# The second product of an MLP by Strassen's scheme, with the squared tiles kept in DRAM

## What is computed

```python
def sq_relu_mlp(h, w1, w2):
    return jnp.square(jax.nn.relu(h @ w1)) @ w2     # h 1024x1024, w1 1024x4096, w2 4096x1024
...
    xl = xl + g2_l * sq_relu_mlp(modulate(rms_norm_2(xl, norm2_g[i]), sh2_l, s2_l), mlp_w1[i], mlp_w2[i])
return rms_norm_2(xl, final_g)
```

## Time and profile before

| | |
|---|---|
| median of 3 runs | 2042.74 us (2037.37 to 2042.86) |
| profiled execution: span, first to last instruction | 2035.5 us |
| TensorE busy | 2002.3 us, 98% of the span |
| VectorE busy | 1062.4 us, 52% |
| ScalarE busy | 814.5 us, 40% |
| GpSimd busy | 775.0 us, 38% |

### The profile page before, as it was taken

How to read it: one execution, slowest core, us unless ns; L and a number is a source line. 1 busy time by engine, 2 the same in 40 slices (tenths; PEclk the granted TensorE clock), 3 DMA queues, 4 the chain that set the end, 5 groups by cost and what they waited for, 6 DMA issues and landing times.

```text
span 2035.5 us, 26356 instructions
## 1 busy us (share of the span) xinstructions
PE 2002.3 (98%) x10210; PEld 1682.8 (83%) x10210; DVE 1062.4 (52%) x1903; ACT 814.5 (40%) x1365; POOL 775.0 (38%) x482
## 2 busy tenths in 40 slices
PE   9999999999999999999999999999999999999997
PEld 7988988988987888888878877788788888888886
DVE  6154455436555465654589978897541211112125
ACT  5423331343434622132365575753544333222311
POOL 4511111112121344353359857794444444222220
PEclk9999999999999999999999999999999999999998
DMA  5301101110112596774345432332223332111112
GB/s 187 104 22 52 46 29 52 48 47 32 48 47 87 182 316 241 244 272 161 110 186 186 175 102 97 96 94 91 92 84 104 98 99 83 50 44 52 52 42 83
DMA packets 69566, 215.64 MB, mean 106 GB/s; under 512 B 7857, under 2 KB 8241, under 8 KB 69313
## 3 DMA queue, kind: packets, MB, share of 16 engines
q1 hardware_dynamic: 55472, 188.26, 27.5%
q10 hardware_dynamic: 13968, 25.70, 3.7%
HBM read 184.56 MB, written 29.36 MB: 105 GB/s over the span
## 4 chain that ended last, share of the span: by engine, by line
PE 60%; DVE 3%; ACT 2%; issue 2%; POOL 1%; POOLq 0%; DVEq 0%; ACTq 0%
PE B L1519 34%; PE B L1698 24%; PE B L1789 1%; DVE HB L2242 1%; POOL WL L2774 0%; PE B L1725 0%; POOL CO L2819 0%; DVE B L2242 0%; DVE RES L2242 0%; DVE TM L2242 0%; ACT CO L2191 0%; PE B L1683 0%; PE B L1772 0%; ACT HB L1914 0%; ACT RES L2146 0%
## 5 line engine op out<-in xcount | busy, mean ns | idle before, releaser
L1519 PE MATMUL B<-HB,WH 128*128 128x512 f32 x2976 | 929.4, 400 | 5.5 <-ACT HB L1914 3.1
L1519 PEld LDWEIGHTS B<-HB,WH 128*128 128x128 f32 x2976 | 546.9, 188 | 124.8 <-issue 15.2
L2774 POOL TENSOR_TENSOR WL<-RAW,WH 128x1024 fp32r<-128x1024 f32 x164 | 394.2, 2407 | 591.2 <-ACT WH L1914 590.1
L1519 PE MATMUL B<-HB,WL 128*128 128x512 f32 x1488 | 562.3, 391 | 1.8 <-POOL WL L2774 1.8
L1914 ACT ACTIVATE WH<-RAW 128x1024 fp32r<-128x1024 f32 x205 | 215.3, 1055 | 454.1 <-DMA RAW<-wall 434.1
L1519 PEld LDWEIGHTS B<-HB,WL 128*128 128x128 f32 x1488 | 279.8, 188 | 62.9 <-POOL WL L2774 3.4
L2772 POOL TENSOR_TENSOR WL<-RAW,WH 128x512 fp32r<-128x512 f32 x82 | 113.5, 1408 | 317.2 <-ACT WH L1914 317.1
L2242 DVE SCALAR_TENSOR_TENSOR RES<-B,modv,RES 128x512 f32<-128x512 f32 x144 | 105.2, 747 | 200.4 <-PE B L1698 176.7
L2242 DVE SCALAR_TENSOR_TENSOR B<-UP,vec,B 128x512 f32<-128x512 f32 x308 | 208.1, 746 | 0.0
L1698 PE MATMUL B<-HIDH,WH 128*128 128x512 f32 x512 | 185.4, 395 | 1.4 <-DVE RES L2242 1.4
L1698 PE MATMUL B<-HIDL,WH 128*128 128x512 f32 x512 | 182.4, 389 | 0.0
(11 more groups left out here) (247 smaller groups left out, 2598.7 us busy)
## 6 DMA issues: line engine op xcount, KB each, us to landing
RAW<-wall SPq DMA_DIRECT2D x204, 512.0 KB, 3.5
...
WH<-parts SPq DMA_DIRECT2D x32, 512.0 KB, 3.2
WL<-parts SPq DMA_DIRECT2D x32, 512.0 KB, 4.1
RES<-xT SPq DMA_DIRECT2D x16, 512.0 KB, 8.3
...
OI<-oscr SPq DMA_DIRECT2D x16, 512.0 KB, 5.2
parts<-WH SPq DMA_DIRECT2D x16, 512.0 KB, 5.2
```

The costliest lines, as they stand in the source:

```text
L1519: i = pe.matmul(bank, a[:, ks], hb(part, k, h), start=k == 0 and n == 0, stop=k == 7 and n == 2)
L2774: i = po.tensor_tensor(lo, raw, hi.bitcast(F32), ALU.subtract)
```

## The change

The hidden tiles of a group form a 2x2 block matrix B: two by two channel tiles, by the two halves of the tokens. A weight unit holds, for each such pair, four 128x128 quarters A. For groups 0 to 6 the product of A and B is made by the Winograd form of Strassen's scheme, with 7 block products (`part`) in place of 8. Group 7 stays as it was.

- `hid` on ScalarE takes the relu into `RL`, which frees the bank, and the square into one of 4 buffers `HR`; `hid_store` sends it to DRAM (`hscr`), a DMA issued by ScalarE. `hid_lo` is gone. All 32 first-product tiles of one half are made, then all 32 of the other, and only then comes the second product of all groups. The last four tiles of the first half (`FILL`) stand beside the norm of the second half, where one group stood.
- `hq_load` on SyncE's queue reads the squares back, 2 MB a group in four DMAs.
- `op_sum` on GpSimd makes the sums of B quarters, 8 a group. `operand` splits each of the 14 operands of a group: high copy on ScalarE, low subtraction on VectorE.
- `w_sum` on VectorE makes four sums of A quarters of each weight unit, 4 instructions of 128x256. ScalarE copies the sums' high part (`SUMH`, 128x1024), GpSimd subtracts the low part (`SUML`, 128x1024), behind the unit's own split.
- `part_out` on VectorE adds each block product, or a running sum of them in its bank, to `RES`: 6 a unit, 24 a group. The second product of the seven stays in a bank of its own (2 to 5) over groups 0 to 6.

```diff
+TERMS = {1: ("A11", "B11"), 2: ("A12", "B21"), 3: ("S4", "B22"), 4: ("A22", "T4"), 5: ("S1", "T1"), 6: ("S2", "T2"), 7: ("S3", "T3")}
+INTO = {1: (0, 0), 2: (0, 0), 6: (0, 1), 3: (0, 1), 5: (1, 1), 7: (1, 1), 4: (1, 0)}
+    plan += [("w1", i, 0) for i in range(4 * HG - FILL)]
+    plan += [("pw2", f, 1) for f in range(8)] + [("w1", i, 0) for i in range(4 * HG - FILL, 4 * HG)]
+    plan += [("w1", i, 1) for i in range(4 * HG)]
+    plan += [("w2", g, j, 2) for g in range(HG) for j in range(4)]
...
+    for n in range(N):
+        if n % 4 == 0:
+            for _ in ahead_of:
+                pass
+            ahead_of = operands_ahead(n // 4 + 1)
+        order = [(n, 1), (n - 1, 7), (n, 5), (n, 2), (n - 1, 4), (n, 6), (n, 3)]
+        for place, (u, m) in enumerate(order):
+            if u >= 0:
+                part(u, m)
+                for w in waiting:
+                    part_out(*w)
+                waiting = [(u, m)]
+            unit_ahead(n, place)
+            at_ = 7 * (n % 4) + place
+            late_slots[0] = at_ >= 24
+            if at_ >= 3 and at_ % 4 != 2:
+                next(ahead_of, None)
...
+                for r in range(2):
+                    for i, (wt, op) in enumerate(((hi, OPH[x]), (hi, OPL[x]), (lo, OPH[x]))):
+                        p = pe.matmul(bank, wt[:, c:c + 128], op[:, :], start=opens and r == 0 and i == 0,
+                                      stop=r == 1 and i == 2, skip_group_check=True)
...
-                ac.activation(BANKS[b], RL[:, :], ACT.Square).then_inc(sig["hid_sq"], 1)
-                copy(HID[i % NH][0][h][:, :], BANKS[b]).then_inc(sig["hid_hi"], 1)
+                ac.activation(RL[:, :], BANKS[b], ACT.Relu).then_inc(taken[b], 1)
+                ac.activation(HR[at_][:, :], RL[:, :], ACT.Square).then_inc(sig["hid_sq"], 1)
+            def hid_store(i, h):
+                n = hid_n[i, h]
+                w.wait_ge(sig["hid_sq"], n + 1)
+                ac.dma_start(hscr[i, :, h * 512:(h + 1) * 512], HR[n % NHR][:, :]).then_inc(sig[f"d_back{n % NHR}"], 16)
...
+            def operand(q, m):
+                x = SLOT_OF[q, m]
+                w.wait_ge(sig["op_hi"], nth["operand", q, m])
+                if m == 5:
+                    w.wait_ge(sig["op_sum"], nth["op_sum", q, 6])
+                elif m == 6:
+                    w.wait_ge(sig["op_sum"], nth["op_sum", q, 4])
+                tt(OPL[x][:, :], raw_operand(q, m), OPH[x][:, :].bitcast(F32), ALU.subtract).then_inc(sig["op_lo"], 1)
+            def w_sum(q, s):
+                w.wait_ge(sig[f"d_raw{q % NW}"], 16 * raw_n[q])
...
+                if s == "S1":
+                    i = tt(two, quarter(raw, "A21"), quarter(raw, "A22"), ALU.add)
...
+            def part_out(g, j2, m):
+                stt(rh(f, h), BANKS[b], modcol[:, 40 + f:41 + f], rh(f, h), ALU.mult, ALU.add).then_inc(taken[b], 1)
...
+                if q in SUMMED:
+                    n = SUMMED[q]
+                    w.wait_ge(sig["s_hi"], n + 1)
+                    po.tensor_tensor(SUML[n % 3][:, :], SUMR[n % 3][:, :], SUMH[n % 3][:, :].bitcast(F32),
+                                     ALU.subtract).then_inc(sig["s_lo"], 1)
+            def op_sum(q, m):
+                to = OPT[SLOT_OF[q, m]][:, :]
+                wait_operand_slot(w, q, m)
+                wait_hq(w, q)
+                if m == 5:
+                    i = po.tensor_tensor(to, hq(q, "B12"), hq(q, "B11"), ALU.subtract)
...
+            def hq_load(q):
+                if q > 1:
+                    w.wait_ge(sig["op_lo"], nth["operand", q - 2, 7])
+                for k, i in enumerate(tiles):
+                    sp.dma_start(HQ[q % 2][k][:, :], hscr[i, :, :]).then_inc(sig[f"d_scr{q % 2}"], 16)
```

More of the change, by code:

```diff
@@ L128, with is_summed, operands_of, operand_slots @@
 AHEAD_UNITS = [u[1:] for u in UNITS if is_ahead(u)]
+def is_summed(unit):
+    return unit[0] == "w2" and unit[1] < LAST
+SUMMED = {q: n for n, q in enumerate(q for q, u in enumerate(UNITS) if is_summed(u))}
+def operands_of(g):
+    if g < LAST:
+        return [(2 * g + r, m) for m in (1, 5, 2, 6, 4, 3, 7) for r in range(2)]
+    return [(2 * g + r, b) for r in range(2) for b in ("B11", "B12", "B21", "B22")]
+def operand_slots():
+    early = list(range(14))
+    late = list(range(14, NS))
+    last_norm = {6, 7, 14, 15}
+    free, place, gone = early + late, {}, {}
+    leaving = []
+    for g in range(HG):
+        for q, m in operands_of(g):
+            ok = [x for x in free if g < LAST or x not in last_norm]
+            if g == LAST - 1:
+                ok.sort(key=lambda x: x not in last_norm)
+            while not ok:
+                x = leaving.pop(0)
+                free.append(x)
+                ok = [x for x in free if g < LAST or x not in last_norm]
+            x = ok[0]
+            free.remove(x)
+            before = [k for k, v in place.items() if v == x]
+            gone[q, m] = before[-1] if before else None
+            place[q, m] = x
+        if g < LAST:
+            leaving += [place[2 * g + r, m] for m in (1, 5, 2, 6, 3, 7, 4) for r in range(2)]
+    return place, gone
+SLOT_OF, BEFORE = operand_slots()
 WALL = list(dict.fromkeys(contents(u) for u in UNITS))
@@ L677, in add_sq, with out_pair @@
             sq["late"].append((which, f, h))
-    def out_pair(what, out, g, j2, last, halves=((0, 1),), between=None):
+    def out_pair(what, out, g, j2, last, between=None):
         j = u_get(what, g, j2, *((2,) if what == "w2" else ()))
@@ L686, in out_pair @@
             gemm(what, j, names, 4, g, f)
+            if between is not None and f % 2 == 0:
+                between()
             if f % 2:
@@ new lines, in make_plan, with part @@
+    late_slots = [True]
+    ahead_of = operands_ahead(0)
+    for i in range(GT, 4 * HG):
+        hidden(i, 1)
+        if i == 4 * HG - 1:
+            while due:
+                next_due()
+        if i > GT + 2:
+            next(ahead_of, None)
+            next(ahead_of, None)
+    for _ in ahead_of:
+        pass
+    window[0] = 0
+    unit_of, writer = {}, P.writer
+    def part(n, m):
+        g, j2 = n // 4, n % 4
+        name = ("part", g, j2, m)
+        if m == 1:
+            unit_of[n] = u_get("w2", g, j2, 2)
+        if m == 2:
+            if g == 0:
+                take(Ring([2 + j2]), "part2", j2)
+        else:
+            take(Ring([n % 2 if m in (1, 6, 7, 4) else 6 + n % 2]), *name)
+        piece("part", g, j2, m, unit_of[n])
+        tick(6 * pace[0])
+        if m == 4:
+            u_done(unit_of.pop(n), *name)
@@ L1129, in make_plan, with last_part @@
+    for _ in ahead_of:
+        pass
+    part(N - 1, 7)
+    for w in waiting:
+        part_out(*w)
+    part_out(N - 1, 7)
+    def last_part():
+        part(N - 1, 4)
+        part_out(N - 1, 4)
+        window[0] = NW
     first_half = []
```

364 lines of the change are left out of this document (243 added, 121 removed).

## The result

| | before | after |
|---|---|---|
| launch time, median | 2042.8 us (2037.37 to 2044.71, 4 runs) | 2061.25 us (2059.16 to 2064.92, 4 runs) |
| ratio | | 1.010, 95% interval 1.0080 to 1.0119 |
| profiled execution: launch, span | span 2035.5 us | 2060.92, span 2058.9 us |
| stretch of the seven groups | 304.6 us (7 x 43.52) | 330.4 us |
| the rest of the span | 1730.9 us | 1728.5 us |

Slower by 1.0%, 18.5 us, where I had forecast 41. The stretch of the changed kernel is counted from the first block product (1667.25) to the first matmul of group 7 (1996.26), and the one block product that stands inside group 7 is added, 1.36 us.

A forecast was written before the change was run, and what follows sets the result against it. TensorE was taken to bound the kernel; VectorE and GpSimd excluding each other would make seven groups 346 us against 304.6, +41 with saved matmuls included. 2035.5 + 41 = 2077 us of span, plus 7.2, gave 2084; range 2030 to 2135.

The forecast's parts named there:

- What bounds the kernel, what is removed: MLP second product: TensorE sets the pace; one matmul in eight goes, 5.44 us a group, 38.1 in all.
- The two together: Second product: VectorE instructions with two SBUF inputs and GpSimd's SBUF reads exclude each other; 39.4 to 58.5 us a group.
- the sign: Whether the whole change makes the launch slower or faster: slower 0.80, faster 0.16.
- Between the bounds: Seven groups of the second product: 51 us a group, some 40 for the last, 346 us against 304.6 before.
- The heavy cycle: Unit of a group with two long GpSimd subtractions, then four operand sums: 15.7 us where TensorE needs 9.52.
- the walk: Step through one group's VectorE and GpSimd instructions in order: units of 9.6, 15.7, 13.2 and 12.5 us, 51 a group.
- the clock as a rival: Second product: TensorE's waits lower its clock for a fifth of the matmuls, adding 27 to 53 us; chance 0.10.
- The rest at nothing: First products, convolution's end, DMA, group 7 and the end: costed at nothing; late units, up to 21 us, only in the range.
- The offset: Whole launch: the median stood 7.2 us above the profiled span, added to 2077 to give 2084 us.
- exclusion: Second product: VectorE stands still for GpSimd's whole SBUF-reading instruction, 20 of GpSimd's 27.2 us a group.
- common path: SBUF access VectorE and GpSimd take in turn: 12.2 plus 27.2, 39.4 us a group; used without gaps, 2014 us, chance 0.10.

The follow-up runs named there:

- v6: Changed kernel with GpSimd's subtractions replaced by memsets and the operand sums left out, so the product isn't computed: 1997.2 us.
- v3: Changed kernel with GpSimd's subtractions and operand sums replaced by memsets of about the same length, so the product isn't computed: 2018.6 us.
- v1: Changed kernel with the low parts of weights and weight sums and the operand sums moved from GpSimd to VectorE: 2043.82 us, 1.0032 of the kernel before.
- v2: Changed kernel with only the low parts of weights and weight sums moved from GpSimd to VectorE: 2057.84 us, 1.0102 of the kernel before.
- v5: Changed kernel with only the operand sums moved from GpSimd to VectorE: 2064.59 us, 1.0129 of the kernel before.
- v12: Changed kernel with only its order changed, operands and operand sums spaced evenly: 2055.76 us, 1.0098 of the kernel before.

## Why the prediction was right, and where it was wrong

*What bounds the kernel, what is removed*: right. With its causes taken away (v6) the stretch is 266.6 us, 38.0 less than 304.6, at 0.2267 us a matmul.

*The two together*: right, and the step on which the sign rested. VectorE ends 0.56 us behind GpSimd's instruction in the changed kernel as in the earlier trace rows, additions stay at 0.74, and memsets on GpSimd, which read nothing, leave `OPL` at 0.69 (v3). The Trainium skill (SBUF — State Buffer, "Who interferes with whom") exempts GpSimd instructions that only write. v3's trace agrees, by its 0.69 us.

*Between the bounds*: right in kind, too large in size; this is the step that failed. 346 us were forecast for the seven groups, 330.4 measured. The heavy cycle was 15.7 and is 15.64, and not by luck: counted from `WL`, the walk had the low part done at 2.95, `SUML` at 5.2 and the next low part at 8.25, and the trace has 2.95, 5.19 and 8.19. The two behind it were walked at 13.2 and 12.5 and are 11.67 and 10.78 (from `WL` to `WL`, at 1743.86, 1755.53 and 1766.31), the one ahead at 9.6 and is 10.0. So a group is 47.9 to 48.5 us in groups 1 to 4 and 49.7 in group 5, not 51: 12.4 us over five groups. Up to 1.8 us a group of this, 9 of the 12.4, can be VectorE's durations, 29.5 us of own work and not 31.3 (0.66 for 0.70, 0.60 for 0.64, 0.33 for 0.34); that is an estimate, and in the heavy cycle, where GpSimd sets most of the time, they changed next to nothing. The rest lies in the two cycles behind it, whose walk isn't written out, so the cause is open in part. What the trace shows is that the four GpSimd instructions of the first of them did not stand in a row: `SUML` ended at 1749.37 and the pair of sums then waited 1.95 us for TensorE:

```profile
1751.33 2.76 POOL L3062 TENSOR_TENSOR OPT<-HQ,HQ 128x512 f32<-128x512 f32 x2 [1.95 <-PE B L1941]
```

Meanwhile VectorE did a weight sum and a low part undisturbed (0.41 and 0.68 us). The second of them has no operand sums at all. Group 0 takes 44.1 and not 51, 6.9 less: its first unit has only five block products, in 6.8 us, and its operands are ready; I had priced it like the others. Group 6 takes 43.6, with the last unit's two late block products in it, against 40. Together 15.7 us less. TensorE stood for 52.6 us of the stretch, a sixth of it and not a quarter, and VectorE's two-input instructions had means of one and a half to two times their minima, not two to three.

*Half clock* is in those 330.4 us with 11.2, and was in none of my terms, so that without it the walk would have been further off, by up to these 11.2. They are an upper bound of what the clock cost: in the heavy cycle VectorE works without a pause from 1784.73 to 1792.69, so that a faster TensorE would have waited for it, and the walk without any clock gave that cycle to 0.1 us. I had the clock as a rival of 27 to 53 us. Its form was right: behind each of the six stops of 3.9 us, from start to start, stand six to thirteen matmuls at the lower level, and seven more behind one of 2.2 us; a fifth of the stretch was too much, it is some 56 matmuls of 1176. The Trainium skill (TensorE: Matmul & The Clock Gate, "HAM oscillation") tells of this pattern, stops that bring the clock down again and again; the trace agrees.

*The rest at nothing*: nearly. The first products run without gaps, store and all (1500 to 1600 us: 100.00 busy). The rest is 2.4 us shorter than before. 1.4 of them are TensorE's one wait for an addition to `RES` in the earlier trace rows, beside the convolution's end, where VectorE now has no such additions. Another 1.6 us are there far ahead of the MLP: the first 5940 matmuls, as many in both kernels, are done at 1043.93 us before and at 1042.29 now. By the 1041.0 to 1047.4 us of all traces that is scatter. Late weight units did not show in the second product.

*The offset*: wrong by 4.9 us. I added 7.2 us between span and median. In all thirteen profiled runs after it, the launch is 1.8 to 2.1 us over the span (2060.92 to 2058.9 here). The profiled execution of before was its quickest run: 2037.37 is 1.9 over 2035.5. The 5 us were scatter of the runs and not a part of the kernel. The kernel before, run again beside the experiments, had 2036.4 to 2039.1; against that the change costs 22 to 25 us, near the 23.4 between the two spans.

In sum: 41.4 us forecast, less 15.6 for the walk and 2.4 for the rest, is a span 23.4 longer, and less the 4.9 of the offset the 18.5 that were measured.

What is left open: how the 46.2 us of exclusion split over weights and operand sums. v1, v2 and v5 move the one, the other or both, but put VectorE's own work in its place, and v2 and v5 show that the halves don't add. Open too is what makes 48 us a group of 39.4 us of common path when the sums are spaced (v12).
